# Turning the gated attention output by DMA transposes of its 16-bit halves in place of TensorE transposes

## The chip, the cores and the metric

The kernel runs on one core of one Trainium2 chip. The metric is the device time of one execution in microseconds; three runs of the kernel before gave 1651.32, 1651.42 and 1652.93, median 1651.42.

## The reference, cut to what matters

A sequence of 4096 rows of width 1024 goes through one block. RMSNorm and one input projection give a pooling branch and a chunked attention branch (8 heads of 64), each with a SiLU gate. The two gated outputs are put side by side, multiplied by the output projection and added to the residual; a last RMSNorm follows.

```python
y_attn = chunked_rel_attention(qh, kh, vh, rel_bias[layer]) * jax.nn.silu(attn_g)
y = jnp.concatenate([y_pool, y_attn], axis=-1)
x = x + jnp.einsum('bse,ed->bsd', y, w_out[layer])
return rms_norm(x, final_norm_gain)
```

Each query row reads its own chunk of 64 keys and the 8 chunks before it. The result has to hold to float32 accuracy, so the kernel splits operands into a high and a low 16-bit half and forms three 16-bit products for each float32 product.

## The kernel before, in words

Three phases follow each other: the `h` phase (normalisation, transposition, values and gates), the `q` phase (pooling branch and its share of the output projection) and the `a` phase (keys, queries, attention, the attention share of the output projection, the last normalisation). The change lies in the `a` phase.

The `a` phase goes over 16 tiles of 256 query rows (`ATILES`; `LAST` is 15), and in each over 8 heads. Every engine runs its own list of work, and semaphores order the lists. `head(t, h)` on TensorE (line 2043) issues, in a fixed order: scores of two key groups, a filler, row maxima of a later head, scores of the third group, the row that holds the maxima, a filler, the value products of the head before, more maxima, perhaps the transposes of the gated output, and a filler. A filler (`other`, line 2017) is one of two kinds. Key and query products for later tiles (`kq_half`, lines 1717 to 1720) fill slots 0 to 6 and 17 to 23 of a tile's 24; the output products of the tile before (`output`, line 1952) fill slots 7 to 16, the first of them at head 2, slot 1. The last tile has no key and query products, and there the output products of tile 14 take slots 7 to 14.

VectorE's `attend` (lines 2190 to 2196) normalises a head's values, applies the gate and writes them in float32 to `y`, which holds 256 query rows x 512 columns with rows on partitions. The output products need them with columns on partitions and as two 16-bit halves. For tile t - 1 that is done in two rounds at heads 0 and 1 of tile t (`round_at`): TensorE transposes four 128x128 float32 blocks into the PSUM bank `tra` (`branch_transposes`, line 2014), ScalarE copies them to 16 bits as the high half (`branch_hi`, line 2077) and VectorE forms the low half (`branch_lo`, line 2164). The last tile transposes its own output in three rounds. The bank `tra` is shared with the row of maxima (`max_rows`, line 1900), whose copy (line 2085) is short.

All loads and stores go out from SyncE's queue in a written order (line 2319 on). At tile t it issues the second half of the values (`load_v`, line 1795) and of the gates (`load_gate`, line 1802), which wait for the last head of tile t - 1; the residual rows of tile t - 1 (`load_residual`, line 2309); the seven operand blocks for tile t + 2 (`load_hop3`, line 1784); keys and queries moved from SBUF to SBUF for heads 0 to 3 of tile t + 1 (`move_k`, `move_q`, lines 1837 and 1826); values and gates for these heads; two stores of finished rows (`store`, line 2313); and the moves for heads 4 to 7.

```python
            def branch_hi(t, r):
                act.wait_ge(A["yt_mm"], 2 * t + r + 1)
                first, end = round_kts(t, r)
                nc.scalar.activation(yT_h[:, first:end, :],
                                     tra[:, 0:(end - first) * AT].rearrange("p (k n) -> p k n", k=end - first),
                                     ACT.Copy, scale=YSCALE).then_inc(A["yth_done"], 1)
```

## Time and profile before

| | |
|---|---|
| median of three runs | 1651.42 us |
| span of the profiled execution, first to last instruction | 1648.8 us |
| TensorE matmul busy | 1609.6 us, 98% |
| VectorE, ScalarE, GpSimd busy | 1063.1, 838.7, 666.8 us |
| DMA | 258.01 MB, mean 156 GB/s |
| granted TensorE clock, mean | 0.998 |

The profiled execution is given by its span; its own time with what lies around the span is not in the profile. Matmuls are pipelined and each one's duration includes a stretch that overlaps the next one's, so what one matmul costs is read from the distance of the starts in order of time, not from its duration.

### The profile page before, as it was taken

What the parts mean: (1) busy time and instruction counts of PE and PEld (TensorE: products, weight loads), DVE (VectorE), ACT (ScalarE), POOL (GpSimd) and SP (SyncE); (2) the same over time, 40 slices, a digit from 0 to 9 for tenths busy, and PEclk for the clock granted to TensorE, in tenths of its full rate; (3) what the DMA queues carried; (4) which work ended last, traced back from release to release, by engine and by line L of the source; (5) the groups of instructions that cost most, each with busy time, mean ns of one, the idle gap of its engine ahead of it and who ended that gap; (6) DMA issues with size and microseconds to landing.
All of it is one profiled execution on the core that took longest, in us unless ns stands there. A gap on an engine that the chain in (4) does not pass through costs nothing. (4 is left out here: it accounts for less than half of the span.)

```text
span 1648.8 us, 44365 instructions
## 1 busy us (share of the span) xinstructions
PE 1609.6 (98%) x17944; PEld 1214.9 (74%) x17944; DVE 1063.1 (64%) x2200; ACT 838.7 (51%) x1589; POOL 666.8 (40%) x718
## 2 busy tenths in 40 slices
PE   7999999999999999999999999999999999999987
PEld 3455455468677777767777998889888898888964
DVE  7976866747565566557346666666666666666665
ACT  6654655522111111112136677776677677676785
POOL 2543433311101111111414555555555555555564
PEclk9999999999999999999999999999999999999999
DMA  7556556473614533552865443444334444344341
GB/s 249 211 192 218 201 206 221 167 280 124 228 64 169 201 128 106 179 192 87 224 222 147 145 124 110 136 140 139 116 118 136 143 136 119 114 138 136 98 142 52
DMA packets 144145, 258.01 MB, mean 156 GB/s; under 512 B 16040, under 2 KB 78008, under 8 KB 141896
## 3 DMA queue, kind: packets, MB, share of 16 engines
q1 hardware_dynamic: 142904, 253.88, 46.4%
q8 instruction: 143, 2.34, 0.6%
q0 software_dynamic: 1040, 1.31, 0.5%
q14 instruction: 58, 0.48, 0.1%
HBM read 151.40 MB, written 83.54 MB: 142 GB/s over the span
## 5 line engine op out<-in xcount | busy, mean ns | idle before, releaser
L2280 POOL TENSOR_TENSOR stages<-stages 128x512 f16<-128x512 f32 (+2 forms) x368 | 364.4, 993 | 350.6 <-ACT stages L2108 350.1
L1717 PE MATMUL bank<-middle,weights 128*128 128x128 f16 x1792 | 310.5, 219 | 1.2 <-DVE entry L1350 0.9
L1720 PE MATMUL bank<-middle,weights 128*128 128x128 f16 x1792 | 310.5, 219 | 0.0
L1719 PE MATMUL bank<-middle,weights 128*128 128x128 f16 x1792 | 310.4, 219 | 0.0
L2102 ACT ACTIVATE stages<-bank,log_ps 128x512 f32<-128x512 f32 (+2 forms) x368 | 221.9, 603 | 159.2 <-PE bank L1975 97.3
L1922 DVE CUSTOM_DVE_ANT_0 stages<-bank,stages 128x640 bf16<-128x640 f32 (+4 forms) x256 | 198.5, 776 | 73.8 <-PE bank L1887 73.5
L1119 PE MATMUL bank<-middle 128*128 128x256 f16 x784 | 213.7, 273 | 0.5 <-DVE stages L1259 0.5
L1122 PE MATMUL bank<-middle 128*128 128x256 f16 x784 | 213.7, 273 | 0.0
L1121 PE MATMUL bank<-middle 128*128 128x256 f16 x784 | 213.7, 273 | 0.0
L2108 ACT ACTIVATE stages<-stages 128x512 f16<-128x512 f32 (+2 forms) x368 | 202.8, 551 | 11.7
L1952 PE MATMUL bank<-entry,stages 128*128 128x512 f16 x768 | 190.8, 379 | 1.1 <-DVE stages L2164 1.1
L1717 PEld LDWEIGHTS bank<-middle,weights 128*128 128x128 f16 x1792 | 175.1, 98 | 2.1 <-issue 1.3
L1719 PEld LDWEIGHTS bank<-middle,weights 128*128 128x128 f16 x1792 | 175.2, 98 | 0.6
L1720 PEld LDWEIGHTS bank<-middle,weights 128*128 128x128 f16 x1792 | 175.1, 98 | 0.0
L1143 PE MATMUL bank<-entry,stages 128*128 128x512 f16 x768 | 169.6, 379 | 0.5 <-DVE middle L1750 0.5
L1972 PE MATMUL bank<-middle 128*128 128x256 f16 (+1 forms) x840 | 161.4, 242 | 2.9 <-DVE middle L2196 1.7
L1425 POOL TENSOR_TENSOR stages<-stages 128x512 f16<-128x512 f32 x32 | 38.2, 1194 | 309.5 <-ACT stages L1204 309.5
L330 PE MATMUL bank<-weights,middle 128*128 128x512 f16 x392 | 148.6, 379 | 3.6 <-DVE stages L695 1.6
L333 PE MATMUL bank<-weights,middle 128*128 128x512 f16 x392 | 148.6, 379 | 0.0
L332 PE MATMUL bank<-weights,middle 128*128 128x512 f16 x392 | 148.6, 379 | 0.0
L1143 PEld LDWEIGHTS bank<-entry,stages 128*128 128x128 f16 x768 | 74.9, 98 | 86.0 <-DVE middle L1750 0.6
L1750 DVE SCALAR_TENSOR_TENSOR middle<-bank,middle 128x256 f32<-128x256 f32 x160 | 67.8, 424 | 101.2 <-PE bank L1720 100.0
(156 smaller groups left out, 3663.4 us busy)
## 6 DMA issues: line engine op xcount, KB each, us to landing
entry<-in_x SPq DMA_DIRECT2D x64, 512.0 KB, 3.7
h_ops<-middle SPq DMA_DIRECT2D x16, 1792.0 KB, 6.2
middle<-h_ops SPq DMA_DIRECT2D x112, 256.0 KB, 5.6
middle<-h_ops SPq DMA_DIRECT2D x49, 512.0 KB, 7.7
middle<-middle SPq DMA_DIRECT2D x384, 64.0 KB, 2.0
residual<-entry SPq DMA_DIRECT2D x32, 512.0 KB, 2.6
out<-entry SPq DMA_DIRECT2D x31, 512.0 KB, 2.6
entry<-residual SPq DMA_DIRECT2D x30, 512.0 KB, 5.1
```

What stands on the lines that cost most here:

```text
L1119: nc.tensor.matmul(bank, wh, hop[:, :, s, 0, kt, :], start=(kt == 0 and s < 4), stop=False, skip_group_check=True)
L1121: nc.tensor.matmul(bank, wh, hop[:, :, s, 1, kt, :], start=False, stop=False, skip_group_check=True)
L1122: mm = nc.tensor.matmul(bank, wl, hop[:, :, s, 0, kt, :], start=False, stop=(kt == 3), skip_group_check=True)
L1143: mm = nc.tensor.matmul(op_bank(n, n2), part, w[:, kt, n2 * 512:(n2 + 1) * 512], start=(kt == 0 and w is wot_h and part is yh), stop=(kt = ...
L1717: nc.tensor.matmul(dst, wh, hop3[:, o, 0, kt, :], start=(kt == 0 and s < 2 and pair == 0), stop=False, skip_group_check=True)
L1719: nc.tensor.matmul(dst, wh, hop3[:, o, 1, kt, :], start=False, stop=False, skip_group_check=True)
L1720: mm = nc.tensor.matmul(dst, wl, hop3[:, o, 0, kt, :], start=False, stop=(kt == 3), skip_group_check=True)
L1922: nc.vector.tensor_tensor_reduce((junk0 if t == 0 and h < 2 else junk2)[:, c:640], wide[:, c:640], bias_q[:, h, c:640], 1.0, -3e38, ALU.ad ...
L1952: mm = nc.tensor.matmul(out_bank(t, i), yh, w, start=(m == 0), stop=(m == 11))
L2102: nc.scalar.activation(p32[g][:, a:b], score_bank(g)[:, a:b], ACT.Exp, bias=log_ps[:, 0:1]).then_inc(A["exp_done"], 1)
L2108: nc.scalar.activation(p_h[:, h % 2, c + a:c + b], p32[g][:, a:b], ACT.Copy).then_inc(A["ph_done"], 1)
L2280: nc.gpsimd.tensor_tensor(p_l[:, h % 2, c + a:c + b], p32[g][:, a:b], p_h[:, h % 2, c + a:c + b], ALU.subtract).then_inc(A["pl_done"], 1)
```

## The change

For tiles 0 to 14 TensorE's transposes go away (`round_at` now answers only for the last tile, which keeps its three rounds). In their place ScalarE makes the high half from `y` in SBUF and VectorE the low half, in two instructions of 256 columns each, into a new SBUF buffer `y16`; then SyncE issues one DMA transpose of 128 partitions x 1024 16-bit elements (256 KB) from `y16` to `yT`. Columns 0 to 255 (heads 0 to 3) are turned at head 5 of the same tile, columns 256 to 511 at head 0 of the next. On SyncE's queue the first lies between the gates for tile t + 1 and the two stores, the second between the gates and the residual loads. The output products wait for both transposes. The reserved scratch for GpSimd's DMA descriptors is set to 4096 bytes (the default is 16384), and the seven semaphores of the operand loads are shared with the phase before.

```diff
@@ -197,6 +198,7 @@
         y = view(RM, 81920, (2, ATTN), F32)
+        y16 = sb("branch_halves", [P, 2, 2, 2, 2 * P], F16)
         res = view(E, 0, (2, D), F32)
...
@@ -209,8 +211,7 @@
         junk0 = view(Z, 18432, (640,), BF16)
-        yT_h = view(Z, 34048, (NKT, AT), F16)
-        yT_l = view(Z, 36096, (NKT, AT), F16)
+        yT = view(Z, 34048, (2, 2, 2, AT), F16)
 
...
@@ -1560,6 +1561,7 @@
         half_stored = sem("a_half_stored")
+        turned = [sem(f"a_turned{r}") for r in range(2)]
         last_loaded = [sem(f"a_last_loaded{s}") for s in range(2)]
...
@@ -1651,9 +1653,17 @@
 
-            if t > 0 and h < 2:
-                return t - 1, h
             return {HALF + 1: (t, 0), HEADS - 1: (t, 1)}.get(h) if t == LAST else None
+
+        def turn_at(t, h):
+
+            if h == 0 and t > 0:
+                return t - 1, 1
+            return (t, 0) if h == HALF + 1 and t < LAST else None
+
+        def turned_part(part, kts):
+            first = kts.start
+            return yT[:, first // 2, part, first % 2:first % 2 + kts.stop - first, :]
 
...
@@ -1696,7 +1706,7 @@
                 if w % 2 == 0:
-                    pe.wait_ge(hop3_loaded[o], 16 * (t + 1))
+                    pe.wait_ge(hop3_loaded[o], 16 + 16 * (t + 1))
                 if w == 0 and s == 0:
...
@@ -1934,7 +1944,11 @@
                 if first == 0:
-                    pe.wait_ge(A["ytl_done"], 2 * t + (1 if t == LAST else 2))
+                    if t == LAST:
+                        pe.wait_ge(A["ytl_done"], 1)
+                    else:
+                        for r in range(2):
+                            pe.wait_ge(turned[r], 16 * (t + 1))
                     if t == 0 and i == 0:
...
@@ -2072,11 +2086,20 @@
             def branch_hi(t, r):
-                act.wait_ge(A["yt_mm"], 2 * t + r + 1)
+                act.wait_ge(A["yt_mm"], r + 1)
                 first, end = round_kts(t, r)
-                nc.scalar.activation(yT_h[:, first:end, :],
+                if r == 0:
+                    act.wait_ge(A["out_mm"], 4 * t)
+                nc.scalar.activation(turned_part(0, slice(first, end)),
                                      tra[:, 0:(end - first) * AT].rearrange("p (k n) -> p k n", k=end - first),
                                      ACT.Copy, scale=YSCALE).then_inc(A["yth_done"], 1)
+
+            def turn_hi(t, r):
+                act.wait_ge(A["ya_done"], 2 * (HEADS * t + HALF * (r + 1)))
+                at_least(act, turned[r], 16 * t)
+                nc.scalar.activation(y16[:, r, 0, :, :].rearrange("p k (j n) -> p k j n", j=2),
+                                     y[:, :, 2 * r * P:(2 * r + 2) * P].rearrange("p j (k n) -> p k j n", k=2),
+                                     ACT.Copy, scale=YSCALE).then_inc(A["yth16_done"], 1)
 
...
@@ -2159,12 +2184,22 @@
             def branch_lo(t, r):
-                dve.wait_ge(A["yth_done"], 2 * t + r + 1)
+                dve.wait_ge(A["yth_done"], r + 1)
                 first, end = round_kts(t, r)
                 nc.vector.scalar_tensor_tensor(
-                    out=yT_l[:, first:end, :], in0=tra[:, 0:(end - first) * AT].rearrange("p (k n) -> p k n", k=end - first),
-                    scalar=YSCALE, in1=yT_h[:, first:end, :],
+                    out=turned_part(1, slice(first, end)),
+                    in0=tra[:, 0:(end - first) * AT].rearrange("p (k n) -> p k n", k=end - first),
+                    scalar=YSCALE, in1=turned_part(0, slice(first, end)),
                     op0=ALU.mult, op1=ALU.subtract).then_inc(A["ytl_done"], 1)
+
+            def turn_lo(t, r):
+                dve.wait_ge(A["yth16_done"], 2 * t + r + 1)
+                for j in range(2):
+                    ins = nc.vector.scalar_tensor_tensor(
+                        out=y16[:, r, 1, :, j * P:(j + 1) * P],
+                        in0=y[:, j, 2 * r * P:(2 * r + 2) * P].rearrange("p (k n) -> p k n", k=2),
+                        scalar=YSCALE, in1=y16[:, r, 0, :, j * P:(j + 1) * P], op0=ALU.mult, op1=ALU.subtract)
+                ins.then_inc(A["ytl16_done"], 1)
 
...
@@ -2191,7 +2226,7 @@
                     dve.wait_ge(gate_loaded[h // HALF], 32 * (t + 1))
-                    at_least(dve, A["yt_mm"], 2 * (t - 1) + 1 + h // HALF)
+                    at_least(dve, A["ytl16_done"], 2 * (t - 1) + 1 + h // HALF)
                 for j in range(2):
...
@@ -2312,6 +2349,12 @@
 
+            def turn(t, r):
+                sp.wait_ge(A["ytl16_done"], 2 * t + r + 1)
+                at_least(sp, A["out_mm"], 4 * t)
+                sp.dma_start_transpose(yT[:, r, :, :, :].rearrange("p a k (j n) -> p (a k j) n", j=2),
+                                       y16[:, r, :, :, :].rearrange("p a k n -> p (a k n)")).then_inc(turned[r], 16)
+
             def load_wob(n):
...
@@ -2327,6 +2370,7 @@
                         sp.wait_ge(A["wob_lo"], NKT)
+                    turn(t - 1, 1)
                     for j in range(2):
...
@@ -2341,6 +2385,7 @@
                 load_gate(sp, t + 1, 0)
+                turn(t, 0)
                 if t > 0:
...
@@ -2402,7 +2447,7 @@
     arrays = {f"in_{k}": np.ascontiguousarray(v) for k, v in arrays.items()}
-    nc = bacc.Bacc("TRN2", target_bir_lowering=False, num_devices=1)
+    nc = bacc.Bacc("TRN2", target_bir_lowering=False, num_devices=1, dynamic_dma_scratch_size=SCRATCH)
     args = [nc.dram_tensor(k, v.shape, mybir.dt.from_np(v.dtype), kind="ExternalInput").ap() for k, v in arrays.items()]
```

## Rows read from the trace of the kernel before

**Rows 1.** The page: span, and busy time and share of each engine
```profile
span 1648.8 us, 44365 instructions
...
PE 1609.6 (98%) x17944; PEld 1214.9 (74%) x17944; DVE 1063.1 (64%) x2200; ACT 838.7 (51%) x1589; POOL 666.8 (40%) x718
```

**Rows 2.** Windows: busy us (count) of each engine, then TensorE's granted clock, DMA share, GB/s
```profile
884.00:1537.00 653.00, 653.00 (x10359) 568.86 (x10357) 417.03 (x1047) 461.03 (x868) 373.61 (x385) 1.00 0.44 131
...
1537.00:1589.00 52.00, 49.36 (x769) 42.23 (x767) 34.44 (x84) 39.16 (x73) 31.78 (x32) 0.99 0.34 103
...
1589.00:1648.00 59.00, 47.14 (x577) 32.94 (x574) 34.88 (x82) 36.70 (x69) 29.88 (x34) 0.96 0.28 95
```

**Rows 3.** TensorE in order of time, head 1 of a tile: start us, us, operation, count
```profile
1246.10 0.44 PE L1887 MATMUL bank<-middle 128*128 128x128 f16 x4
...
1246.38 0.60 PE L2014 MATMUL bank<-ident,middle 128*128 128x128 f32 x4
...
1246.82 0.22 PE L1717 MATMUL bank<-middle,weights 128*128 128x128 f16 x1
```

**Rows 4.** All engines in order of time, head 0 of the same tile
```profile
1239.34 0.47 DVE L2196 SCALAR_TENSOR_TENSOR middle<-bank,rc,middle 128x64 f32<-128x64 f32 x2
...
1239.98 0.58 ACT L2077 ACTIVATE stages<-bank 128x512 f16<-128x512 f32 x1
...
1240.59 0.69 DVE L2164 SCALAR_TENSOR_TENSOR stages<-bank,stages 128x512 f16<-128x512 f32 x1
```

**Rows 5.** SyncE's queue in the same tile
```profile
1241.50 0.91 SPq L2309 DMA_DIRECT2D entry<-residual  x2
...
1242.45 8.24 SPq L1784 DMA_DIRECT2D middle<-h_ops  x7
```

**Rows 6.** The first work that needs what these bring: output products, residual, next key product
```profile
1251.02 1.02 PE L1952 MATMUL bank<-entry,stages 128*128 128x512 f16 x4
...
1255.68 0.69 DVE L2208 SCALAR_TENSOR_TENSOR entry<-bank,entry 128x512 f32<-128x512 f32 x1 [1.26 <-PE bank L1952]
...
1272.21 0.38 ACT L1727 ACTIVATE middle<-bank 128x256 f32<-128x256 f32 x1 [1.33 <-PE bank L1720]
```

**Rows 7.** The page, DMA issues: KB each, median us from issue to landing
```profile
middle<-h_ops SPq DMA_DIRECT2D x112, 256.0 KB, 5.6
...
middle<-middle SPq DMA_DIRECT2D x384, 64.0 KB, 2.0
```

**Rows 8.** Answer on one line of SyncE: ns of issue, least, median, most
```profile
L1826 SPq DMA_DIRECT2D middle<-middle x192: 462/597/1665, 821.4 to 1594.4; - x192
```

**Rows 9.** SyncE, then TensorE, in order of time in the last tile
```profile
1597.03 1.07 SPq L1802 DMA_DIRECT2D middle<-gates  x2
...
1600.91 0.27 PE L1900 MATMUL bank<-ident,m 128*128 128x128 f16 x2 [0.52 <-DVE stages L2164]
...
1601.04 1.45 PE L1952 MATMUL bank<-entry,stages 128*128 128x512 f16 x6
```

**Rows 10.** Groups of instructions by line: busy us, mean ns, idle before
```profile
L493 ACT ACTIVATE middle<-stages 128x512 f16<-128x512 f32 x28 | 16.1, 618 | 0.0
...
L1363 DVE SCALAR_TENSOR_TENSOR weights<-stages,weights 128x256 f16<-128x256 f32 x32 | 24.9, 778 | 9.0 <-ACT weights L1218 9.0
```

**Rows 11.** Head 5 of the tile: VectorE and SyncE in order of time
```profile
1271.93 1.28 DVE L2217 SCALAR_TENSOR_TENSOR entry<-entry,stat 128x1024 f32<-128x1024 f32 x1
...
1274.22 0.42 DVE L1750 SCALAR_TENSOR_TENSOR middle<-bank,middle 128x256 f32<-128x256 f32 x1 [1.01 <-PE bank L1720]
...
1273.24 7.67 SPq L2313 DMA_DIRECT2D out<-entry  x2
```

**Rows 12.** The one DMA of GpSimd and the first user of what it brings
```profile
L1453 POOL DMA_DIRECT2D stages<-bias_by_query x1: 1053/1053/1053, 803.7 to 803.7; - x1
...
DMA to landing us min/median/max: 16.0/16.0/16.0
...
L1909 DVE MEMSET stages<- x1: 485/485/485, 834.4 to 834.4; 64x512 bf16 x1
```

More of the change, by code:

```diff
@@ L18 @@
 ALU = mybir.AluOpType
+SCRATCH = 4096
 ACT = mybir.ActivationFunctionType
@@ L1551, in build @@
             max_mm max_done mrow_mm mrow_done st_mm bias_done exp_done ph_done pl_done
-            pv_mm rc_done ya_done yt_mm yth_done ytl_done ss_done ms_done rstd_done fin_done""".split()
+            pv_mm rc_done ya_done yt_mm yth_done ytl_done yth16_done ytl16_done ss_done ms_done rstd_done fin_done""".split()
         A = {n: sem("a_" + n) for n in names}
         wob_loaded = [sem(f"a_wob_loaded{n}") for n in range(NKT)]
-        hop3_loaded = [sem(f"a_hop3_loaded{s}") for s in range(PRODUCTS)]
+        hop3_loaded = entry_loaded
         moved_k = [sem(f"a_moved_k{s}") for s in range(2)]
@@ L1896, in max_rows @@
             if h >= 2 and round_at(t, h - 2):
-                of, r = round_at(t, h - 2)
-                pe.wait_ge(A["ytl_done"], 2 * of + r + 1)
+                _, r = round_at(t, h - 2)
+                pe.wait_ge(A["ytl_done"], r + 1)
             for j in range(2):
@@ L1946, in output @@
                 elif t == LAST:
-                    pe.wait_ge(A["ytl_done"], 2 * t + first // 3)
+                    pe.wait_ge(A["ytl_done"], first // 3)
                 for m in range(first, end):
                     kt, p = m // 3, m % 3
-                    yh = (yT_l if p == 2 else yT_h)[:, kt, j * P:(j + 1) * P]
+                    yh = yT[:, kt // 2, 1 if p == 2 else 0, kt % 2, j * P:(j + 1) * P]
                     w = (wob_l if p == 1 else wob_h)[:, kt, n2 * 512:(n2 + 1) * 512]
@@ L2010, in branch_transposes @@
                 if t == LAST and r > 0:
-                    pe.wait_ge(A["ytl_done"], 2 * t + r)
+                    pe.wait_ge(A["ytl_done"], r)
                 for q in range(2 * (end - first)):
@@ L2145, in head @@
                     branch_hi(*round_at(t, h))
+                if turn_at(t, h):
+                    turn_hi(*turn_at(t, h))
                 other(t, h, 2)
@@ L2249, in head @@
                     branch_lo(*round_at(t, h))
+                if turn_at(t, h):
+                    turn_lo(*turn_at(t, h))
                 other(t, h, 2)
```

## The prediction, written before the result was known

> **What bounds the kernel now.** I read the page first, then the windows of the attention phase, then three short pieces of the order in time: TensorE around a round of transposes, all engines at head 0 of a tile, SyncE's queue behind it. The page gives TensorE 98% of the span and no other engine over 64% [rows 1]. The windows say where that holds: from 884 to 1537 us, which is tiles 1 to 13, TensorE is busy for all of 653.00 us, with the clock granted at 1.00 (2.4 GHz), ScalarE for 461.03, VectorE for 417.03, GpSimd for 373.61 [rows 2]. There the time is TensorE's list of work and nothing else. From 1537 (most of tile 14) it is busy 49.36 us of 52, and in the last tile and the tail 47.14 of 59: there several engines wait for each other by turns. So an instruction taken from TensorE counts in full for thirteen tiles, nearly so in the fourteenth, and the last has to be looked at by itself.
>
> **What goes.** A round is four transposes. They start at 1246.38, and the next product starts at 1246.82: 0.44 us a round, 0.11 each, though their drawn length is 0.60 because the pipeline's tail overlaps the next work [rows 3]. The products before them start at 1246.10, four of them in 0.28 us, so no gap stands ahead of the round either. A tile has two rounds, 0.88 us; the change touches fifteen tiles' output, 30 rounds, 13.2 us in all. Thirteen tiles in the full stretch give 13 x 0.88 = 11.4. In tile 14 I count 0.88 x 49.36/52 = 0.8. The two rounds in the last tile are handled below.
>
> **What comes on ScalarE and VectorE.** ScalarE's copy of 512 columns reads SBUF in place of PSUM: 618 ns on average for such a form, against 0.58 now [rows 4, 10]. VectorE's one instruction of 0.69 us [rows 4] becomes two of 256 columns from SBUF. The trace has this very form at 778 ns a piece, in a stretch where GpSimd works beside it [rows 10]; half of the present 0.69 is the lower end, so the pair costs 0.7 to 1.6, and I take 0.9. Neither is on the path in the full stretch: it adds at most 1.8 us per tile of 50 to engines with over 190 us idle in 653 [rows 2]. Instruction by instruction: at head 0 the high half waits for the gated values, done at 1239.34 + 0.47 = 1239.8, when ScalarE is still occupied until 1239.98; it ends at 1240.6. The low half follows at 1240.6 and ends at 1241.5, where the old one ended at 1241.3 [rows 4]. Behind it on VectorE is the take of a key product, which has another product's time before its result is wanted. At head 5 the pair pushes the final scaling of 1.28 us by 0.9, and the next instruction there had stood idle for 1.01 [rows 11]. If that cover were gone, VectorE would be late by under 1 us once a tile, and TensorE, which runs up to two heads behind on its maxima, would feel a part of it. I cost it at nothing.
>
> **What comes on SyncE and the DMA engines.** This is the step that decides. The trace has no DMA transpose. Call X the time from its turn on the queue to its landing. The turn of the second half starts when the gate copies are out and the low half is done, both at 1241.5 [rows 5]. The output products that need it start at 1251.02 [rows 6]. The slack is 9.5 us, and since TensorE would come there 0.88 earlier, a transpose with X up to 8.6 costs nothing. Beyond that each tile changes by -0.88 + (X - 8.6), and breaks even at X = 9.5. The first half is turned at head 5, over 20 us before its use.
>
> X from the nearest rows: a move of 64 KB within SBUF lands after 2.0 us, which is the lower end for 256 KB; 256 KB loads from DRAM land after 5.6, in bursts of seven that share the engines [rows 7]. Eight blocks of 128x128 one behind the other, each with the 2.0 - 0.6 = 1.4 us that a 64 KB move takes beyond its issue (0.6 us, [rows 8]), give 8 x 1.4 + 0.6 = 11.8, the upper end. I take X = 5, of which 2 on the queue: the bytes are those of the 5.6 us row, and a transpose must cut its source into more pieces than a plain move.
>
> Of these 2 us everything behind it on SyncE is late. The residual loads, issued 1241.5 to 1242.4 [rows 5], land some 5 us after issue and are first read at 1255.68 [rows 6]: 8 us to spare. The seven operand loads run to 1250.7 and are needed for the key product whose copy runs at 1272.21 [rows 5, 6]. At head 5 the two stores move by 2 us; the first of them leaves at 1273.24 and the queue's next work is 8 us later [rows 11]. All hidden.
>
> The smaller scratch touches only GpSimd's one DMA: issued at 803.7, landed 16.0 us later at 819.7, first used at 834.4, so it may take 14 us longer at no cost [rows 12]. The shared semaphores cost nothing.
>
> Two rules disagree on X. The Trainium skill, "VectorE: DVE Perf Modes", section "The three transpose paths", gives 1309 ns for one 128x128 transpose by DMA; eight of them in series would be an estimate of 10.5 us, and the sum below would come out near +21 us. The Trainium skill, "Advanced Engine Details and Errata", section "X-Bar Transpose (TRN2)", says that transposes run at 350 to 400 GB/s, which would be an estimate of 0.7 us for 256 KB and leave the sum as it is. No row here can choose between them.
>
> **The last tile.** The heads are short, since no key products fill them. SyncE's gate copies end at 1598.10, and the output products start at 1601.04, right after a wait of 0.52 us for VectorE's low half [rows 9]. That wait and the two rounds go (1.4 us), but with X = 5 the transpose lands at 1603.1, so the output starts 2.1 us later than now, and TensorE's list stands still behind it. I count the 2.1 in full. In general this place adds X - 2.9.
>
> **The sum.** -11.4 - 0.8 + 2.1 = -10.1 us. The profiled span of 1648.8 us becomes 1638.7; the median of the runs is 2.6 above the span, so 1651.4 - 10.1 = 1641.3.
>
> **The rivals.** From the same terms, with 14 tiles for the steady part: the change in all is -12.2 + X - 2.9 up to X = 8.6, and 14 x (X - 9.5) + X - 2.9 beyond.
>
> Rival one, slower: the blocks go one after another. X is then 11.8, TensorE stands at head 2 of every tile for 3.2 us, and the change is 14 x 2.3 + 8.9 = +41, or 1692 us. For it: a transpose is no plain copy, and nothing in the trace shows its rate. Against it: in this trace 64 KB and 256 KB land within 2.0 and 5.6 us [rows 7], so the engines serve many pieces side by side. It decides from X = 9.3 on, where the sum passes what can be told from zero. The first of the two rules of the Trainium skill named above is this rival's, with a slightly lower price.
>
> Rival two, no change that can be told (within 0.2%, 3.3 us, which is about what a measurement of this kernel can separate): X between 8.8 and 9.3, so that the wait eats the saving; 1651. The window is narrow, but a mixture of a shorter X and a last tile that loses more would look the same.
>
> Rival three, also slower: not the transfer but the issue is long. SyncE then holds the queue, the transpose lands late and the residual loads come after it; those need their 8 us of spare, so this acts from about the same X. With 10 us on the queue and 2 to land X is 12 and the time some 1695. For it: one issue in the trace took 1.67 us at most and 0.46 at least for the same 64 KB [rows 8], so issue time is not a constant. Against it: no issue here comes near 10.
>
> That the work is hidden anyway, so that removing it gives nothing, is excluded for tiles 1 to 13 by 653.00 of 653 [rows 2].
>
> **Chances and range.** Forecast 0.68, rival two 0.09, rival one 0.19, rival three 0.04. Within the forecast X runs from 2 to 8.6, which gives -13.1 to -6.5, and if the last tile's wait gains another 1 us, -14: its own range is 1637 to 1645. With rival two and the near part of the slower cases the range is 1636.5 to 1662. Faster by over 0.2%: 0.68; within: 0.09; slower: 0.23.
>
> **What would show it.** TensorE's busy time falls by 11 to 13 us and stays equal to the window from tile 1 to 13; no wait of the output products (now line 1952) for a DMA there; each of these tiles 0.88 us shorter than before, from the start of the output products in one to the next. SyncE shows the transpose at 2 us or so, and its landing 3 to 7 us after. In the last tile the output products wait some 3 us for the DMA. I am wrong if TensorE stands before the first output product in every tile; the length of that wait is X - 8.6. A wait of VectorE for the residual would point to rival three.

## The result, and the profile after

The changed kernel takes 1654.03 us (median of 20 runs, 1652.76 to 1657.52) against 1652.12 for the kernel before in the same comparison (20 runs, 1649.60 to 1652.93): a ratio of 1.0016, 95% interval 1.0009 to 1.0023. The forecast was 1641.3. So the change costs some 2 us, less than the 0.2% named as the least that counts, and the 10 us that it was to bring are missing.

The time lies within the stated range of 1636.5 to 1662, but by luck: the part of the range above 1651 was there for a transpose of 8.8 us and more, and that isn't what happened. The outcome is the one that rival two names (no change that can be told, chance 0.09), reached in another way.

Two single executions stand far outside all others, 2381.62 us in experiment 7 and 1845.64 in experiment 4; the ratios below leave them out, and without them the medians given there, 1655.29 and 1641.91, would be 1655.00 and 1641.83.

First the page of the changed kernel, which answers to [rows 1]:

```profile
span 1652.8 us, 44242 instructions
...
PE 1601.0 (97%) x17824; PEld 1203.6 (73%) x17824; DVE 1097.6 (66%) x2230; ACT 837.6 (51%) x1589; POOL 672.1 (41%) x718
```

TensorE lost 120 matmuls (30 rounds of four), and its busy time fell by 8.6 us; the span grew by 4.0. VectorE has 30 instructions more, as the diff says (60 for 30), but 34.5 us more of busy time: over 1 us for each pair in place of the 0.2 forecast. The windows of the changed kernel, which answer to [rows 2] (the last is longer, since the span is):

```profile
884.00:1537.00 653.00, 647.00 (x10296) 560.76 (x10294) 448.28 (x1077) 462.74 (x872) 376.87 (x385) 1.00 0.49 142
1537.00:1589.00 52.00, 48.96 (x764) 41.59 (x761) 37.05 (x88) 37.57 (x71) 31.81 (x31) 1.00 0.43 101
1589.00:1652.00 63.00, 46.05 (x584) 32.11 (x584) 36.17 (x85) 37.71 (x71) 31.37 (x36) 0.96 0.31 103
```

TensorE was busy for 653.00 of 653 us; now it is for 647.00. Where work was taken away, TensorE began to stand. Its waits from 884 to 1590 us in the changed kernel name the place (total us, times, longest):

```profile
PE bank L1727 <- DVE middle L1760: 6.4, 14, 1.2
```

L1727 is a key product's first matmul, and L1760 is VectorE's take of an earlier product from its PSUM bank. It is the very instruction that stands behind the low half in VectorE's list; before the change no such wait existed. The order of time in the changed kernel shows the cause at head 0 of a tile (first six rows), the same pair at head 5 (next three) and the last tile (last two); the third row is what GpSimd does next:

```profile
1243.56 2.12 POOL L1773 TENSOR_TENSOR middle<-middle 128x1024 f16<-128x1024 f32 x1
...
1243.86 2.92 DVE L2198 SCALAR_TENSOR_TENSOR branch_halves<-middle,branch_halves 128x256 f16<-128x256 f32 x2
...
1245.64 2.15 POOL L2317 TENSOR_TENSOR stages<-stages 128x256 f16<-128x256 f32 x2
...
1246.70 0.93 DVE L1760 SCALAR_TENSOR_TENSOR middle<-bank,middle 128x256 f32<-128x256 f32 x2
...
1246.80 1.27 SPq L2355 DMA_TRANSPOSE stages<-branch_halves  x1
...
1247.17 0.23 PE L1727 MATMUL bank<-middle,weights 128*128 128x128 f16 x1 [0.37 <-DVE middle L1760]
...
1274.82 0.80 DVE L2198 SCALAR_TENSOR_TENSOR branch_halves<-middle,branch_halves 128x256 f16<-128x256 f32 x2
1275.54 1.27 DVE L2252 SCALAR_TENSOR_TENSOR entry<-entry,stat 128x1024 f32<-128x1024 f32 x1
...
1275.64 1.27 SPq L2355 DMA_TRANSPOSE stages<-branch_halves  x1
...
1600.61 1.28 SPq L2355 DMA_TRANSPOSE stages<-branch_halves  x1
...
1603.98 1.24 PE L1966 MATMUL bank<-entry,stages 128*128 128x512 f16 x5 [1.88 <-issue]
```

The same two instructions take 0.80 us at head 5 and 2.92 at head 0, where GpSimd has just begun one instruction of 2.12 us. Two takes then run back to back from 1246.70 (x2: the second one had become due too), and TensorE starts 0.37 late. This counts from the drawn end of the product ahead; from start to start, which is what a tile's length is made of, it is 0.54. Earlier in the trace, in tile 1, the wait is 1.23 us. The durations of all 60 low halves and of all 30 transposes in the changed kernel (ns least, median, most; then us from issue to landing, for the transposes):

```profile
L2198 DVE SCALAR_TENSOR_TENSOR branch_halves<-middle,branch_halves x60: 409/802/2126, 875.3 to 1597.3; 128x256 f16<-128x256 f32 x60
...
L2355 SPq DMA_TRANSPOSE stages<-branch_halves x30: 1258/1268/1945, 876.4 to 1600.6; - x30
...
DMA to landing us min/median/max: 3.1/3.1/5.3
```

So X, which the prediction called the deciding step, is 3.1 us, below the 5 taken and far from the 8.6 at which it would cost anything in a full tile by the prediction's count. The mechanisms of all three rivals fall with it.

**Where the time is, tile by tile.** The distance from the first output product of one tile to that of the next is the time of a tile. "Again" is the kernel before in a later profile (experiment 8 says why it is the fairer partner).

| us | before | before again | changed |
|---|---|---|---|
| span's start to the first output product of tile 1 | 893.68 | 897.09 | 898.65 |
| tile 1 to 2 | 47.50 | 47.49 | 47.44 |
| each of the 12 after it | 51.64 | 51.64 | 51.30 |
| tile 14 to the last tile | 40.19 | 39.26 | 42.24 |
| from there to the end | 47.73 | 47.74 | 48.86 |
| span | 1648.8 | 1651.2 | 1652.8 |

A tile should have become 0.88 us shorter and became 0.34 shorter; the beginning and the end both became longer.

### The profile page after: what moved, and what is told of

The parts are those of the page before. It is cut to its first block and busy times, and to the rows that moved or that the text cites. A ratio compares the mean times of both kernels' runs of the same rounds, so it can differ in the third digit from the quotient of the medians.

```text
span 1652.8 us, 44242 instructions
## 1 busy us (share of the span) xinstructions
PE 1601.0 (97%) x17824; PEld 1203.6 (73%) x17824; DVE 1097.6 (66%) x2230; ACT 837.6 (51%) x1589; POOL 672.1 (41%) x718
## 5 line engine op out<-in xcount | busy, mean ns | idle before, releaser
L2317 POOL TENSOR_TENSOR stages<-stages 128x512 f16<-128x512 f32 (+2 forms) x368 | 368.8, 1006 | 348.4 <-ACT stages L2131 348.2
L1727 PE MATMUL bank<-middle,weights 128*128 128x128 f16 x1792 | 311.9, 220 | 7.6 <-DVE middle L1760 6.4
L1727 PEld LDWEIGHTS bank<-middle,weights 128*128 128x128 f16 x1792 | 175.5, 98 | 10.9 <-DVE middle L1760 8.8
L1989 PE MATMUL bank<-middle 65*128 65x128 f16 (+1 forms) x616 | 129.9, 243 | 0.0
```

Source lines behind the costliest of these rows:

```text
L1727: nc.tensor.matmul(dst, wh, hop3[:, o, 0, kt, :], start=(kt == 0 and s < 2 and pair == 0), stop=False, skip_group_check=True)
L2317: nc.gpsimd.tensor_tensor(p_l[:, h % 2, c + a:c + b], p32[g][:, a:b], p_h[:, h % 2, c + a:c + b], ALU.subtract).then_inc(A["pl_done"], 1)
```

## The experiments

**1 and 2: is it VectorE's place in the order, or the form of its instruction?** In the first the order is changed: at head 0 the take goes ahead of the low half.

```diff
-                if turn_at(t, h):
+                if turn_at(t, h) and h > 0:
                     turn_lo(*turn_at(t, h))
                 other(t, h, 2)
+                if turn_at(t, h) and h == 0:
+                    turn_lo(*turn_at(t, h))
```

> At head 0 VectorE's two low-half instructions stand behind the take of the key product instead of ahead of it. Theory A (in the changed kernel these two wait for GpSimd's instruction of 2.1 us, 2.92 us in all, and the take queued behind them comes late, so that TensorE waits 0.54 us in each tile): TensorE's wait for the take goes, tiles are 50.76 us apart instead of 51.30, and the time falls by about 7 us, from 1654.0 to 1647. The pair itself may still be long. Theory B (the lost time is the DMA transposes disturbing other transfers or SyncE's queue): no change, 1654, tiles stay at 51.30.

Measured: 1646.79 us (1644.61 to 1647.97), ratio to before 0.9963 (0.9950 to 0.9975). Every full tile takes 50.76 us, which is 51.64 less 0.88 exactly. The wait L1727 for L1760 is gone from TensorE. VectorE at head 0 in this kernel:

```profile
1239.36 0.43 DVE L1760 SCALAR_TENSOR_TENSOR middle<-bank,middle 128x256 f32<-128x256 f32 x1 [0.19 <-PE bank L1730]
1239.70 2.46 DVE L2198 SCALAR_TENSOR_TENSOR branch_halves<-middle,branch_halves 128x256 f16<-128x256 f32 x2
1242.09 0.41 DVE L1760 SCALAR_TENSOR_TENSOR middle<-bank,middle 128x256 f32<-128x256 f32 x1
```

The pair is still long, 2.46 us, but nobody waits for it. In the second the order stays as in the changed kernel, and GpSimd's instruction of 128x1024 waits at head 0 until the low half is done.

```diff
                     if split_at(t, h):
+                        if h == 0:
+                            pool.wait_ge(A["ytl16_done"], 2 * t)
                         kq_lo(pool, split_at(t, h))
```

> GpSimd's 1024-column instruction at head 0 waits until VectorE's low half is done; nothing else is changed. If the two engines exclude each other (theory A), the pair takes 0.8 us at head 0 as it does at head 5, TensorE's wait for the take is gone or below 0.3 us, and the time is 1647 to 1650 (GpSimd's result comes 0.9 us later, which may be felt). If the form or the strided pattern is slow by itself at head 0 (theory C), the pair stays at 2.9 us and the time rises, since GpSimd now starts later: 1656 or more.

Measured: 1646.52 us (1645.76 to 1647.66), ratio 0.9963 (0.9949 to 0.9976), 0.5 us under the 1647 to 1650 expected, tiles of 50.76 us again. VectorE and GpSimd at head 0 in this kernel:

```profile
1239.12 0.76 DVE L2198 SCALAR_TENSOR_TENSOR branch_halves<-middle,branch_halves 128x256 f16<-128x256 f32 x2
1239.80 0.42 DVE L1760 SCALAR_TENSOR_TENSOR middle<-bank,middle 128x256 f32<-128x256 f32 x1
...
1239.96 2.13 POOL L1773 TENSOR_TENSOR middle<-middle 128x1024 f16<-128x1024 f32 x1 [1.09 <-DVE branch_halves L2198]
```

```profile
L2198 DVE SCALAR_TENSOR_TENSOR branch_halves<-middle,branch_halves x60: 410/425/961, 874.9 to 1588.8; 128x256 f16<-128x256 f32 x60
```

The same form on the same data takes 0.76 us a pair, 0.425 a piece at the median, once GpSimd does not run beside it. That the form is slow in itself is refuted. The difference of 2.92 - 0.76 = 2.16 us is close to the length of GpSimd's long instruction, but that instruction had only 1243.56 + 2.12 - 1243.86 = 1.82 us left when the pair began. The other 0.34 fits a wait of the second piece for the short GpSimd instruction behind the long one (the third row of the changed kernel above); in experiment 1 the same sum holds, 0.76 + 1.37 left + 0.33 = 2.46.

**3: is it GpSimd's instruction as a whole, or the traffic of both?** The same subtraction on GpSimd in two instructions of 512 columns, VectorE in the order of the changed kernel.

```diff
-            nc.gpsimd.tensor_tensor(nat_of(w, 1), cs_flat(), nat_of(w, 0), ALU.subtract).then_inc(A["nat_lo"], 1)
+            for half in range(2):
+                cols = slice(half * 512, (half + 1) * 512)
+                ins = nc.gpsimd.tensor_tensor(nat_of(w, 1)[:, cols], cs_flat()[:, cols], nat_of(w, 0)[:, cols], ALU.subtract)
+            ins.then_inc(A["nat_lo"], 1)
```

> The changed kernel with GpSimd's 1024-column instruction split into two of 512 columns, nothing else. If VectorE's two-SBUF-operand instruction waits for GpSimd's whole instruction (theory A), its first instruction at head 0 waits for the end of the first half only: the pair is 1.8 to 2.4 us instead of 2.9 us, depending on who goes next, and TensorE's wait shrinks from 0.54 us to 0.0 to 0.3. If the two engines share in smaller portions, the pair keeps its 2.9 us.

Measured: 1649.12 us (1646.44 to 1650.35), ratio 0.9978 (0.9969 to 0.9987), tiles of 50.81 us. The two engines at head 0, from this kernel's order of time:

```profile
1240.82 2.44 DVE L2201 SCALAR_TENSOR_TENSOR branch_halves<-middle,branch_halves 128x256 f16<-128x256 f32 x2
...
1240.51 2.46 POOL L1775 TENSOR_TENSOR middle<-middle 128x512 f16<-128x512 f32 x2
```

The bytes are the same, the pair is 0.48 us shorter (2.44, just above the 1.8 to 2.4 expected), and the two GpSimd pieces together take 2.46 us in place of 2.13; what two pieces would take undisturbed wasn't measured, so how much of this is waiting is open. VectorE's longest single piece falls from 2.13 to 1.38 us. Half a microsecond was enough for TensorE's waits on L1760 to fall from 6.4 to 0.7 us in all. This fits two engines of which each waits out a whole instruction of the other, and not two that share in small portions, for which the pair was expected to keep its 2.9 us.

**4: what does the rest of the change cost?** Nothing is turned for tiles 1 to 14: the halves aren't made and no transpose runs, so their output products read tile 0's data (this is left out of the computation).

```diff
         def turn_at(t, h):
-            if h == 0 and t > 0:
+            if h == 0 and t == 1:
                 return t - 1, 1
-            return (t, 0) if h == HALF + 1 and t < LAST else None
+            return (t, 0) if h == HALF + 1 and t == 0 else None
...
```

> Leaves out the turning of tiles 1 to 14 altogether (no halves, no DMA transpose, no TensorE transposes; the output products read what tile 0 left). It prices what TensorE's rounds are worth with nothing put in their place. By the prediction's step (0.88 us a tile) tiles are 50.76 us apart, and the time is 1643 to 1645, tile 0's loss being kept. If the distance of the starts understates or overstates the cost of a round, the tile distance differs: 50.4 if a round costs its drawn 0.60.

Measured: 1641.91 us, ratio 0.9935 (0.9921 to 0.9948); tiles of 50.76, first output product at 897.85, 38.31 from tile 14 to the last tile, 47.73 behind it. The full tiles are as in experiments 1 and 2: with the take in front, the halves, the transposes and the queue time cost nothing there at all. The floor without any turning is 4.9 us under experiment 1, and this lies at the end: 42.43 - 38.31 = 4.1 in the interval, and 50.47 - 47.73 = 2.7 behind it, less 0.3 at the beginning, makes 6.6 in the spans. (The spans differ by more than the medians because the profiled execution of experiment 1, at 1647.97, was its slowest.) The time is 1 us under the 1643 to 1645 expected, in which a loss of tile 0 was kept that experiments 6 and 8 do not find.

**5: the last tile.** On top of experiment 1, the second half of tile 14 alone is transposed by TensorE, at head 1 of the last tile.

```diff
+        BY_TENSOR = [(14, 1)]
+        BY_TENSOR_AT = {(15, 1): (14, 1)}
...
         def round_at(t, h):
+            if (t, h) in BY_TENSOR_AT:
+                return BY_TENSOR_AT[t, h]
...
```

> The take first, and of the ends only the second half of tile 14 goes back to TensorE, at head 1 of the last tile; tile 0 as in the change. It separates the two ends. If the wait for the DMA in the last tile costs what was read (interval 42.4 against 38.3 with nothing turned), the interval falls to 39 to 40 and the time to 1643.5 to 1644.5; tile 0's loss of some 3.5 us stays. If the interval does not move, the last tile waits for something else.

Measured: 1641.95 us (1641.37 to 1642.54), ratio 0.9935 (0.9922 to 0.9949); 39.59 from tile 14 to the last and 47.73 behind it. One transpose of thirty costs 4.8 us: 42.43 - 39.59 = 2.8 before the output products and 50.47 - 47.73 = 2.7 behind them. The interval came out as expected (39 to 40), the time 1.5 us under the 1643.5 expected at least, for the same reason as in experiment 4.

**6: both ends by TensorE.** Experiment 1 with tiles 0 and 14 transposed by TensorE as before; thirteen tiles are turned by DMA.

```diff
+        BY_TENSOR = [(0, 0), (0, 1), (14, 0), (14, 1)]
+        BY_TENSOR_AT = {(1, 0): (0, 0), (1, 1): (0, 1), (15, 0): (14, 0), (15, 1): (14, 1)}
...
```

> The take first at head 0 (as in the first experiment), and the two ends by TensorE as before the change: both halves of tile 0 at heads 0 and 1 of tile 1, both halves of tile 14 at heads 0 and 1 of the last tile. DMA turns tiles 1 to 13 only. Theory A with the ends as priced so far: tiles 1 to 13 give 13 x 0.88 less the two rounds of tile 0 that stay, the first output product of tile 1 is back near 894 with no stretch at 1.2 GHz before it, the last tile's interval is 40.2 instead of 42.4. Time 1640 to 1642, 11 us under the kernel before. If the ends have nothing to do with it, 1646.8 as in the first experiment.

Measured: 1641.64 us (1641.14 to 1642.17) against 1652.82 for the kernel before beside it, ratio 0.9933 (0.9921 to 0.9946). This is the fastest version, 11.2 us under the kernel before: 13 x 0.88 = 11.4, the first term of the prediction's sum. Against the previous experiment it gains nothing that can be told: tile 0 turned by DMA costs nothing. One part of what was expected missed: the first output product came at 896.93, not near 894, with a stretch of low clock ahead of it.

**7: does the first tile's turn cost?** In the changed kernel the first half of tile 0 is turned at head 0 of tile 1, together with the second.

```diff
-            return (t, 0) if h == HALF + 1 and t < LAST else None
+            return (t, 0) if h == HALF + 1 and 0 < t < LAST else None
...
+                if t == 1 and h == 0:
+                    turn_lo(0, 0)
...
```

> Only tile 0's first half is turned at head 0 of tile 1 instead of head 5 of tile 0. Theory D (the extra work at head 5 of tile 0, where TensorE already waits for others, makes it idle a little more, and the clock granted there then falls from 2.4 to 1.2 GHz for 6.8 us, which costs 3.4 us and the idle time): the stretch at 1.2 GHz is gone, the first output product of tile 1 starts near 895 instead of 898.6, and the time is 1650 to 1651. Rival: the fall of the clock has nothing to do with where this half is turned, and the time stays at 1654.

Measured: 1655.29 us, ratio 1.0015 (1.0006 to 1.0024): no better than the change itself, so what was expected of it missed. In its profile the first output product did come early, at 895.33, and a low clock at the beginning was absent; but the end had one, and the tail was 50.46 us. What looked like an effect of the first tile's turn is taken up next:

**8: is a stretch of low clock the kernel's or the run's?** The kernel before was profiled twice more, unchanged.

> The kernel before, profiled again. Theory D (the stretch at 1.2 GHz near 880 us is brought by the work that the change adds to tile 0) says: full clock up to tile 13, the first output product of tile 1 near 893.7, as in the first profile. Theory E (the clock falls in this weakly loaded stretch by chance of the run, whatever the kernel) says: about as often as not a stretch of 3 to 10 us at 1.2 GHz near 880 us, and then the first output product near 896 to 897.

> The same again, since theory E is about how often: with both profiles at full clock theory D gains, with one or both showing the stretch it falls.

Measured: 1653.02 and 1652.62 us, ratios 1.0007 (0.9996 to 1.0018) and 1.0002 (0.9991 to 1.0013). The window from 870 to 890 us (length, TensorE's busy us; the third number from the end is its granted clock) of the first profile of before, of the second, of experiment 6 and of experiment 7:

```profile
870.00:890.00 20.00, 16.37 (x275) 15.14 (x273) 13.89 (x48) 12.72 (x28) 8.16 (x10) 1.00 0.44 105
```

```profile
870.00:890.00 20.00, 16.69 (x239) 15.31 (x237) 13.11 (x46) 12.25 (x26) 7.79 (x8) 0.83 0.36 89
```

```profile
870.00:890.00 20.00, 16.69 (x237) 15.30 (x235) 12.95 (x45) 12.17 (x26) 7.94 (x9) 0.83 0.37 88
```

```profile
870.00:890.00 20.00, 14.15 (x233) 12.87 (x230) 15.66 (x46) 11.85 (x26) 8.45 (x10) 1.00 0.41 101
```

The same kernel shows 1.00 in one profile and 0.83 in the next two (6.8 us at 1.2 GHz), and experiment 6, whose tile 0 is as before, has 0.83. The stretch isn't caused by the turn of tile 0. The executions of the kernel before that were run beside these point to how often it comes: three of 15 have a mean clock of 0.999 and take 1649.63 to 1650.07 us, the other twelve 0.996 or 0.997 and 1651.29 to 1653.03. Whether the change makes the stretch longer (10.2 us in the profiles of five of the experiments, none of them of the kernel before) is not shown. The first profile of before was one without it, with a span 2 to 2.4 us shorter; hence the second as partner in the table.

**9: what would a longer X cost?** On top of experiment 1, each transpose is issued twice, the second behind the landing of the first.

```diff
-                sp.dma_start_transpose(yT[:, r, :, :, :].rearrange("p a k (j n) -> p (a k j) n", j=2),
-                                       y16[:, r, :, :, :].rearrange("p a k n -> p (a k n)")).then_inc(turned[r], 16)
+                for again in range(2):
+                    sp.dma_start_transpose(yT[:, r, :, :, :].rearrange("p a k (j n) -> p (a k j) n", j=2),
+                                           y16[:, r, :, :, :].rearrange("p a k n -> p (a k n)")).then_inc(turned[r], 16)
+                    if not again:
+                        sp.wait_ge(turned[r], 32 * t + 16)
...
```

> The take first, and every DMA transpose is issued twice, the second after the first has landed, so that X is about 6.3 us instead of 3.1 and twice the bytes go through the engines. In the first experiment the transpose starts 6.6 us ahead of the output products. If the transfer is off the path with that slack, tiles stay 50.76 apart and only the last tile grows by 3 us: 1649 to 1650. If the DMA transposes were disturbing other work (theory B), twice of them must show: tiles further apart by the share that theory gives them, 0.5 us or more.

Measured: 1662.22 us (1661.00 to 1662.70), ratio 1.0056 (1.0044 to 1.0069). Seven tiles in the middle still take 50.75 to 50.77 us; five others, towards the two ends, 51.02 to 51.98; tile 1 to 2 takes 48.29 in place of 46.61, tile 14 to the last 47.44 in place of 42.43, and the first output product comes at 900.38 in place of 897.59. SyncE's queue, and TensorE's waits from 884 to 1590 us:

```profile
1249.21 4.32 SPq L2358 DMA_TRANSPOSE stages<-branch_halves  x2
```

```profile
PE bank L1966 <- issue: 6.7, 6, 2.5
```

The total was expected at 1649 to 1650 and missed by 12 us. X here is at least twice 3.1, some 6.3 us, and the slack isn't the prediction's 8.6: from the issue at 1249.21 to the output products, which start at 1255.76, it is 6.5 in this tile (7.1 in the changed kernel, 1246.80 to 1253.91). In the tiles that became longer, the output products come up to 7.7 us behind the issue, so the two transposes took longer than the slack; these waits make 6.7 us, and the beginning has 2.8. In the last tile, where 3 us were expected, the double turn costs 5.0: the one at head 5 holds the queue, so that the last turn starts 2.7 later, and the output products come 2.3 later behind it. What stands is the reasoning of the prediction: within the slack a transfer costs nothing (seven tiles at 50.76 with twice the transposes), beyond it TensorE stands.

## Why the prediction was wrong, point by point

The prediction's terms against the second profile of before, in us of the span:

| term | forecast | measured |
|---|---|---|
| TensorE's rounds, tiles 1 to 13 | -11.4 | -11.4 |
| VectorE's pair, the same tiles | 0 | +7.4 |
| VectorE's pair in tile 1, ahead of the first output product | 0 | +1.2 |
| rest of the beginning | 0 | +0.3 |
| tile 14 and the last tile's wait | -0.8 + 2.1 | +3.0 |
| tail (the last store's landing) | 0 | +1.1 |
| sum | -10.1 | +1.6 |

The first row is 13 intervals as experiment 1 has them (12 x 0.88, and 47.49 - 46.61); the second is what the changed kernel has over it from the first output product of tile 1 to that of tile 14 (663.1 - 655.7); the others are differences of the table of tiles.

**The rounds: right.** 0.44 us a round from start to start [rows 3] gave 0.88 a tile, and five kernels (experiments 1, 2, 4, 5 and 6) show 51.64 become 50.76. That a matmul's drawn length of 0.60 was not taken was worth 0.32 us a tile.

**The step that failed** is "What comes on ScalarE and VectorE", with its end: "I cost it at nothing." It fails in three places. The pair was taken at 0.9 us and is 2.92 at head 0. The answer stood in the trace of before: [rows 10] gave 778 ns as a mean, and that mean hides two prices. The line of its durations says so (the first row, ns least, median, most, from an answer on this line in the kernel before), and the second row, from before's order of time, is GpSimd's long instruction, which begins 0.26 us ahead of the old low half of [rows 4]; the third is the take behind it:

```profile
L1363 DVE SCALAR_TENSOR_TENSOR weights<-stages,weights x32: 414/426/1379, 466.8 to 784.0; 128x256 f16<-128x256 f32 x32
```

```profile
1240.33 2.13 POOL L1763 TENSOR_TENSOR middle<-middle 128x1024 f16<-128x1024 f32 x1
...
1241.20 0.42 DVE L1750 SCALAR_TENSOR_TENSOR middle<-bank,middle 128x256 f32<-128x256 f32 x1
```

The median piece took 0.43 us and the longest 1.38. The old low half, with PSUM as one of its inputs, took its 0.69 right beside GpSimd; the new one has both inputs in SBUF. The range for the pair, 0.7 to 1.6, came from the mean doubled, where the price is 0.8 plus what is left of GpSimd's instruction, and a part of its next one for the second piece. These rows point to the inputs as what decides, and the take behind the old low half, with one input in PSUM too, took its usual 0.42 beside the same GpSimd instruction; no experiment changed the inputs alone. Second, the take was said to have "another product's time before its result is wanted"; the product waited 0.37 us for it, and the tile lost 0.54. Third, the text did say what would happen without cover, though of head 5 and not of head 0: VectorE "late by under 1 us once a tile", of which TensorE "would feel a part". VectorE is late by 2.0 us (2.92 for 0.9), and the part that TensorE feels is 0.54; it was given no chance and no place among the rivals.

The Trainium skill has this in "SBUF — State Buffer", section "SBUF: two separate sides": VectorE with two SBUF inputs and a GpSimd instruction that reads SBUF share one pair of ports, held exclusively for a whole instruction, the other blocking fully. An estimate by that rule, with the durations of this trace, is 0.8 + 1.8 left of GpSimd's = 2.6 us at head 0 if only the first piece waits; the trace has 2.92, and experiments 2 and 3 agree with the rule (0.76 without GpSimd beside it; with halves of its instruction, a shorter pair).

**X: on the right side.** 5 taken, 3.1 measured, with 1.27 on the queue where 2 was taken. Both ends, 2.0 and 11.8, hold it, and rivals one, two and three needed 8.8 and more. (Rival two's remark, that a shorter X with a last tile that loses more would look the same, has its share in the result, but not the pair of VectorE, which is the largest term.) The residual loads, the operand loads and the stores are late by 1.3 us in a full tile and nobody waits (experiment 1's 50.76), so this step is confirmed in the full stretch. Of the two rules of the Trainium skill that the prediction weighed, neither price is what a transfer costs here: by 1309 ns a block in series ("VectorE: DVE Perf Modes", section "The three transpose paths") X would be 10.5, and by 350 to 400 GB/s ("Advanced Engine Details and Errata", section "X-Bar Transpose (TRN2)") the data would move in 0.7, while 256 KB in the 3.1 - 1.27 = 1.8 us behind the issue are some 145 GB/s. (The prediction says that 0.7 would leave its sum as it is; by its own formula an X of 0.7 makes the sum -14.4.)

**The last tile: place right, size not.** With X = 3.1 the prediction's terms give -0.8 + 0.2 for the interval from tile 14 to the last tile; it is 2.05 longer than in the first profile of before. Counted from tile 14's output products (1560.85 there, 1561.74 in the changed kernel), the turn starts at 38.87 us, where the gate copies had ended at 37.25, and the output products come 3.37 behind it in place of 2.94: 1.6 + 0.4. The transfer itself lands after 3.3 us here. Of the 1.6, 0.7 comes from the transpose of head 5 (1.27 us at 1583.48), which now stands ahead of the stores, moves, loads and gate copies: from there to the turn the queue has no gap over 0.4. The prediction looked at the queue behind head 5 in a full tile, where the next work is 8 us later [rows 11], and took it for the last one. The rest of the 1.6 is the moves and copies themselves, which take longer in some profiles, of the kernel before too. The first two rows are the second profile of before, the third is the changed kernel:

```profile
1601.42 1.07 SPq L1802 DMA_DIRECT2D middle<-gates  x2
...
1603.49 1.45 PE L1952 MATMUL bank<-entry,stages 128*128 128x512 f16 x6
...
1599.68 0.82 SPq L1812 DMA_DIRECT2D middle<-gates  x2
```

In the second profile of before the gate copies end at 1602.49, only 1.0 us ahead of the output products. So the slack of 2.9 was itself read from an execution in which this queue was early and TensorE late: that profile has 3.4 us at 1.2 GHz in tile 14, which the second hasn't, and its interval is 0.9 longer. That 0.9 is the remainder of the 3.0 in the table. And the -0.8 of tile 14 has no place beside this wait: the interval now ends with the queue and the transfer, and what TensorE saves before it, it waits. Experiment 5 prices the whole at 4.8 us in the times, with the tail.

**The tail** of +1.1 in the changed kernel wasn't foreseen. It lies behind all computation: from the last tile's first output product to the issue of the last two stores both kernels take 44.56 us. Then the last store lands after 3.1 us in place of 2.0 (first the kernel before, then the changed one):

```profile
L2355 SPq DMA_DIRECT2D out<-entry x2: 332/332/333, 1645.6 to 1646.3; - x2
DMA to landing us min/median/max: 2.0/2.0/2.0
...
L2400 SPq DMA_DIRECT2D out<-entry x2: 332/332/332, 1648.5 to 1649.2; - x2
DMA to landing us min/median/max: 2.0/2.6/3.1
```

It is 3.1 in the six profiles in which the second half of tile 14 is turned by DMA, and 2.0 to 2.1 in the six in which it isn't (the three of before and experiments 4, 5 and 6). That it hangs on this one transpose is what these profiles show; how, 45 us later, stays open. In experiment 1 the tail is 2.7 longer: 1.1 of it is the same, and 1.6 are the price of 3.4 us at 1.2 GHz right behind TensorE's wait, where the second group of output products comes 4.11 us behind the first in place of 2.49.

**The base.** The prediction put the median 2.6 us above the span. In the changed kernel the profiled execution took 1654.62 for a span of 1652.8, so 1.8. The first profile of before was therefore some 0.8 us quicker than the median of its runs, and the stretch of low clock near 880 us, which most executions have, wasn't in what the prediction read. The forecast is the median less 10.1, so this does not move it; the median itself came out 0.7 higher in the larger comparison.

**Signs that it named.** "TensorE's busy time falls by 11 to 13 us and stays equal to the window": 8.6 us, and 6 us short of the window; this is the sign that showed the error first. "Each of these tiles 0.88 us shorter": 0.34. No wait of the output products for a DMA in tiles 1 to 13: right. "In the last tile the output products wait some 3 us for the DMA": 1.88, right in kind.

## What to carry to other kernels

When an operand moves from PSUM to SBUF, ask what GpSimd runs at that moment: a VectorE instruction with two SBUF inputs may wait out the whole of it, and the mean of a form hides this, so read its least, median and most. Before an edit is costed at nothing, look at the instruction that is queued behind it and count the time until somebody wants that one; here moving a single take ahead of the pair was worth some 7 us. A change that pays in the full stretch need not be made at the ends: there a wait that the full stretch would hide can count, and leaving the old way for one transpose in the last tile was worth 4.8 us. Read the slack at such a place from more than one execution: here it was 2.9 us in one profile of the kernel before and 1.0 in the next.

## What was not expected of the hardware

A DMA transpose of 256 KB of 16-bit data from SBUF to SBUF, eight blocks of 128x128 in one instruction, holds SyncE's queue for 1.27 us and lands 3.1 us after its issue (median of 30; 5.3 at most, at head 5 of the last tile). That is less than the 5.6 us of a 256 KB load from DRAM here.

The last store, 256 KB, lands after 2.0 us in the six profiles without a DMA transpose of the second half of tile 14, and after 3.1 in the six with it, though some 45 us lie between them.

GpSimd pays as well: in experiment 1 the two GpSimd instructions behind its long one take 2.15 us together, against 1.79 in experiment 2, where VectorE is done before.

Stretches of 3.4 to 10.2 us at 1.2 GHz come in places where TensorE stands often, and not in each execution of the same kernel: the profiles of the kernel before have none at 880 us, then 6.8, then 6.8. Two profiles of one kernel differ by 2.4 us in span for it, more than the change under study is worth.
